# A two-layer hybrid diffusion backbone on one core: where the sliding heads' results are copied, how the weights lie in DRAM, and where the differential heads are normed

## What is computed

```
# one layer
h  = rmsnorm(x) * (1 + sc1) + sh1                 # modulation from silu(c) @ w_ada
p  = h @ w_in                                     # 1024 x 2304, nine pieces of 256 columns
ya = window attention, 8 heads of 64, GQA (2 kv heads), band of +-128 keys + 256 context keys + a sink
yb = gate * conv3(gate * p)                       # short convolution
yd = (softmax(q0 k0) - lam * softmax(q1 k1)) @ v  # 4 differential heads, 2 x 32 wide, over all keys
yd = rmsnorm(yd over its 64 columns, per head and token) * subln * (1 - lam_init)
x  = x + g1 * (concat(ya, yb, yd) @ w_out)
h2 = rmsnorm(x) * (1 + sc2) + sh2
x  = x + g2 * moe(h2)     # 16 experts, each takes its top 64 latent (32 context) tokens, SwiGLU, 3 x 4 MB
```

## Time and profile before

| | us |
|---|---|
| median of 3 runs | 2289.03 (2286.83 to 2295.98) |
| the profiled execution, as timed | 2285.29 |
| its span in the profile | 2283.5 |
| layer 0: attention steps | about 327 to 545 |
| layer 0: output projection to routing | about 565 to 701 |
| layer 0: experts | about 709 to 1247 |
| layer 1: W steps | about 1511 to 1618 |
| layer 1: experts | about 1739 to 2246 |

### The profile page before, as it was taken

One profiled execution on the slowest core, in us unless ns is written; L12 is line 12 of the kernel. 1 busy time (PEld: TensorE's weight loads), 2 busy tenths in 40 slices (PEclk: granted clock), 3 DMA queues, 4 the chain that ended last, 5 costly groups with the idle time before them and its releaser, 6 DMA issues.

```text
span 2283.5 us, 31609 instructions
## 1 busy us (share of the span) xinstructions
PE 1857.2 (81%) x13298; PEld 971.5 (43%) x13298; DVE 576.8 (25%) x1219; ACT 345.0 (15%) x753; POOL 260.4 (11%) x374
## 2 busy tenths in 40 slices
PE   4799978876976999999997689877785877777772
PEld 2677535564442444444333577456452222222220
DVE  1311236545233111111111221464333111101111
ACT  1210005453120000000000211255220000000001
POOL 1000004200000111211211000140000111101101
PEclk8999987798987999999999799799987999999997
DMA  9324880000235999999998612100134999999995
GB/s 331 106 93 166 313 331 1 1 1 29 83 129 188 380 391 384 390 385 389 385 390 315 226 56 74 37 1 1 47 138 186 391 390 397 396 392 391 396 402 198
DMA packets 170899, 530.85 MB, mean 232 GB/s; under 512 B 11780, under 2 KB 32544, under 8 KB 170784
## 3 DMA queue, kind: packets, MB, share of 16 engines
q1 hardware_dynamic: 150688, 480.28, 54.8%
q0 software_dynamic: 17488, 48.51, 7.4%
q10 hardware_dynamic: 2608, 0.35, 0.1%
HBM read 506.03 MB, written 23.07 MB: 232 GB/s over the span
## 4 chain that ended last, share of the span: by engine, by line
PE 58%; DMA 23%; DVE 10%; SPq 3%; ACT 3%; issue 2%; POOL 0%; ACTq 0%; DVEq 0%; POOLq 0%
PE psum L1156 12%; DMA ring<-in_w_gate 8%; DMA ring<-in_w_down 7%; PE psum L1089 6%; PE psum L1159 6%; DMA ring<-in_w_up 5%; PE psum L872 5%; PE psum L908 5%; PE psum L992 5%; PE psum L950 5%; DVE smx L1373 3%; PE psum L1150 3%; PE psum L1035 3%; SPq L472 3%; PE psum L826 2%
## 5 line engine op out<-in xcount | busy, mean ns | idle before, releaser
L1150 PE MATMUL psum<-ring,arena 128*64 128x512 f32 x1536 | 369.3, 607 | 118.2 <-DMA ring<-in_w_gate 48.7
L1156 PE MATMUL psum<-ring,arena 128*32 128x512 f32 x3072 | 403.0, 596 | 7.6 <-DVE arena L1506 2.2
L1150 PEld LDWEIGHTS psum<-ring,arena 128*64 128x64 f32 x1536 | 98.2, 137 | 366.8 <-issue 171.6
L1159 PE MATMUL psum<-ring,arena 128*32 128x256 f32 x3072 | 237.3, 380 | 0.0
L1159 PEld LDWEIGHTS psum<-ring,arena 128*32 128x32 f32 x3072 | 101.0, 110 | 230.3 <-issue 230.3
L794 ACT ACTIVATE arena<-psum 128x768 f32<-128x768 f32 (+1 forms) x32 | 22.5, 704 | 1018.3 <-PE psum L1159 522.2
L1373 DVE TENSOR_REDUCE smx<-psum 128x1 f32<-128x768 f32 (+4 forms) x160 | 120.7, 761 | 159.8 <-PE psum L1005 102.1
L731 ACT ACTIVATE arena<-psum,smx 128x768 f32<-128x768 f32 (+4 forms) x160 | 119.8, 751 | 266.3 <-DVE smx L1373 266.2
L1089 PE MATMUL psum<-ring,arena 128*128 128x512 f32 x320 | 144.1, 611 | 19.4 <-DVE arena L1421 19.4
L992 PE MATMUL psum<-arena 64*128 64x256 f32 (+3 forms) x640 | 119.9, 499 | 35.9 <-ACT arena L731 34.6
L1527 DVE SCALAR_TENSOR_TENSOR arena<-psum,gcur,arena 128x512 f32<-128x512 f32 x32 | 24.0, 750 | 460.3 <-PE psum L1159 233.3
(11 more groups left out here) (223 smaller groups left out, 1587.8 us busy)
## 6 DMA issues: line engine op xcount, KB each, us to landing
ring<-in_w_gate SPq DMA_DIRECT2D x128, 1024.0 KB, 4.7
ring<-in_w_up SPq DMA_DIRECT2D x128, 1024.0 KB, 18.5
ring<-in_w_down SPq DMA_DIRECT2D x128, 1024.0 KB, 20.0
ring<-in_w_ada SPq DMA_DIRECT2D x48, 1024.0 KB, 7.0
ring<-in_w_in SPq DMA_DIRECT2D x18, 1024.0 KB, 14.4
ring<-in_w_out SPq DMA_DIRECT2D x8, 1024.0 KB
arena<-residual POOLq DMA_DIRECT2D x14, 512.0 KB, 5.9
residual<-arena POOLq DMA_DIRECT2D x10, 512.0 KB, 2.9
```

Of the source, the lines that this page charges most:

```text
L1150: ins = mm(psum[64 * n:64 * n + 64, b * 512:(b + 1) * 512], lhs(k), w[:, n * 512:(n + 1) * 512], start=k == 0, stop=k == KD - 1)
L1156: ins = mm(psum[r0:r0 + 32, b * 512:(b + 1) * 512], lhs(k)[:, 32 * g:32 * g + 32], w[:, n * 512:(n + 1) * 512], start=k == 0, stop=k == KD ...
L1159: ins = mm(psum[32 * j:32 * j + 32, (b + 1) * 512:(b + 1) * 512 + 256], lhs_c(k), w[:, j * 256:(j + 1) * 256], start=k == 0, stop=k == KD - 1)
```

## The change

Three edits, and helpers for them.

- `by_partition` lays out `w_gate`, `w_up`, `w_down`, `w_out`, `w_ada` and `w_in` in DRAM before the launch, so that a unit's 8 KB for one partition are one run. The units, their order and the ring are as before.
- `mixed` of a W step moves from the end of DVE's iteration to its head.
- The norm of the differential heads goes into the W steps. POOL squares the differential results (1536 or 1024 columns) once all D copies are made. In `values` of W2 PE multiplies each block of squares by `halves`, now 128 x 2, so that tokens lie on partitions and a head's sum is one column (12 or 8 products); DVE copies the 24 or 16 columns, ACT takes the root, DVE the reciprocal. From W5 on, each of 2 x nq(l) steps broadcasts one block's gains through two small products and DVE applies them in `mixed`, just ahead of the copy (`dnorm`). What stood between attention and output projection for it is gone; the projection waits for `dnorm` instead of `dsub`.

```
+def by_partition(w, rows, cols=None):
+    k, n = w.shape[-2:]
+    cols = cols or n
+    lead = w.shape[:-2]
+    w = w.reshape(*lead, k // (rows * P), rows, P, n // cols, cols)
+    w = np.moveaxis(w, -2, -5) if cols < n else w[..., 0, :]
+    return np.ascontiguousarray(np.swapaxes(w, -3, -2))
...
+    SUMS_AT, GAIN_AT = 2, 5
+    def gain_chunk(l, st):
+        c = st.i - 4 * nq(l) - GAIN_AT
+        return divmod(c, 2) if st.kind == "W" and 0 <= c < 2 * nq(l) else None
+    def sums_here(l, st):
+        return st.i - 4 * nq(l) == SUMS_AT
... POOL, after its part of the D steps
+            pool.wait_ge(*L("mix", 2 * nq(l)))
+            pool.tensor_tensor(sqd[:, :, 0:tq], hT[:, 6:8, 0:tq], hT[:, 6:8, 0:tq], ALU.mult).then_inc(L["dsq"], 1)
... ACT, in iteration i behind the copy of the turned probabilities; its square and roots behind the steps are gone
+                    if i >= 5 and sums_here(l, steps[i - 5]):
+                        act.wait_ge(*L("dss", 1))
+                        act.activation(dms[:, 1, 0:nq(l)], dms[:, 0, 0:nq(l)], ACT.Sqrt, bias=eps[:]).then_inc(L["drt"], 1)
... PE, in values(st)
+                if sums_here(l, st):
+                    pe.wait_ge(*L("dsq", 1))
+                    for t in range(nq(l)):
+                        for cc in range(2):
+                            mm(psum[:, a0 + 256 + 4 * t + 2 * cc:a0 + 256 + 4 * t + 2 * cc + 2], sqd[:, cc, toks(t)],
+                               halves[:], start=True, stop=True)
+                if gain_chunk(l, st):
+                    t, cc = gain_chunk(l, st)
+                    pe.wait_ge(*L("dsr", 1))
+                    for h in range(2):
+                        mm(psum[64 * h:64 * h + 64, a0 + P:a0 + 2 * P],
+                           dms[:, 2, t, cc, h:h + 1].broadcast_to([P, HEAD]), ident[:], start=True, stop=True)
... PE, ahead of the output projection
-            pe.wait_ge(*L("dsub", 1))
+            pe.wait_ge(*L("dnorm", 2 * nq(l)))
... DVE, in mixed(st), ahead of its copy
+                if sums_here(l, st):
+                    dve.tensor_copy(dms[:, 0, 0:nq(l)]..., psum[:, a0 + 256:...]).then_inc(L["dss"], 1)
+                if gain_chunk(l, st):
+                    t, cc = gain_chunk(l, st)
+                    stt(hT[:, 6 + cc, toks(t)], hT[:, 6 + cc, toks(t)], sublc[:, l:l + 1], psum[:, a0 + P:a0 + 2 * P],
+                        ALU.mult, ALU.mult).then_inc(L["dnorm"], 1)
... DVE, head of iteration i
+                if i >= 5 and steps[i - 5].kind == "W":
+                    mixed(steps[i - 5])
+                if i >= 7 and sums_here(l, steps[i - 7]):
+                    dve.wait_ge(*L("drt", 1))
+                    dve.reciprocal(dms[:, 2, 0:nq(l)], dms[:, 1, 0:nq(l)]).then_inc(L["dsr"], 1)
... DVE, end of iteration i
-                if i >= 5 and steps[i - 5].kind == "W":
-                    mixed(steps[i - 5])
```

More of the change, by code:

```diff
@@ L200, in ada_units @@
     def ada_units(l, g):
-        v = w_ada[l].rearrange("(h k p) n -> h p k n", p=P, k=4)
-        return [(v[h, :, :, g * 512:(g + 1) * 512], 4) for h in range(2)]
+        return [(w_ada[l, g, h], 4) for h in range(2)]
     def win_units(l):
-        v = w_in[l].rearrange("(k p) n -> p k n", p=P)
         order = [0, 1, 2, 6, 7, 8, 3, 5, 4]
-        return [(v[:, :, 256 * j:256 * j + 256], 8) for j in order]
+        return [(w_in[l, j], 8) for j in order]
     def wout_units(l):
-        v = w_out[l].rearrange("(h k p) n -> h p k n", p=P, k=2)
-        return [(v[h], 2) for h in range(4)]
+        return [(w_out[l, h], 2) for h in range(4)]
     ADA_REST = [(0, g) for g in range(4, 12)] + [(l, g) for l in range(1, DEPTH) for g in range(12)]
@@ L339, in signals @@
         s |= dict.fromkeys("AV mix".split(), 6 * n)
+        s |= dict(dnorm=2 * n)
         s |= dict.fromkeys("cu cuc cy".split(), 2)
-        s |= dict.fromkeys("dsq dss drt dsub asub aexp aff aT pad rows ri".split(), 1)
+        s |= dict.fromkeys("dsq dss drt dsr asub aexp aff aT pad rows ri".split(), 1)
         s |= dict.fromkeys("xt xm xs gc silu he th hs yg".split(), NE)
@@ L464, in _ @@
                 n += 1
[L465 removed]
+            wv = [w[l] for w in (w_gate, w_up, w_down)]
             def load_matrix(which, expert, e, m0):
@@ L1057, in _ @@
                 ins.then_inc(L["gx"], 1)
[L1058 to L1063, removed]
             pe.wait_ge(*L("gxe", 1))
@@ L1204, in _ @@
         dlink(dve, dve.memset(halves[:], 0.0))
-        for h in (0, 64):
-            dve.memset(halves[h:h + 64, h:h + 64], 1.0 / HEAD)
+        for h in range(2):
+            dve.memset(halves[64 * h:64 * h + 64, h:h + 1], 1.0 / HEAD)
         dve.wait_ge(s_pack, 1)
@@ L1562 @@
     arrays = {f"in_{n}": np.ascontiguousarray(inputs[n]) for n in _INS}
+    for n in ("w_gate", "w_up", "w_down", "w_out"):
+        arrays[f"in_{n}"] = by_partition(inputs[n], 2)
+    arrays["in_w_ada"] = by_partition(inputs["w_ada"], 4, 512)
+    arrays["in_w_in"] = by_partition(inputs["w_in"], 8, 256)[:, :, 0]
     shape = inputs["x"].shape
```

28 lines of the change are left out of this document (9 added, 19 removed).

## The result

| | median, us | lowest to highest |
|---|---|---|
| before, 4 runs | 2292.22 | 2286.83 to 2295.98 |
| changed, 4 runs | 2220.84 | 2219.71 to 2223.30 |

The ratio is 0.9692 with an interval of 0.9667 to 0.9717, some 71 us. The profiled execution of the changed kernel was timed at 2219.7 us, its span is 2217.9. In the page after, these lines show most of it: first the chain's shares by engine, then packets and the SP queue (q1: packets, MB, share of 16 engines). DVE holds 7% of the chain (10% before), SP's issuing of loads (SPq) 0% (3% before), and q1 has 65952 packets for the same 480 MB; before it had 150688.

A forecast was written before the change was run, and what follows sets the result against it. PE bounds layer 0's experts, loads layer 1's, DVE's late copy the W steps. Savings 20.5 + 27.4 + 17.4 = 65.3 us give 2220 from the profiled 2285.3, 2223.7 from the median; forecast 2222, range 2203 to 2243.

The forecast's parts named there:

- rival A: All weight loads: they stay at their rate, limited by something other than runs; 2239 us, chance 0.22 together with D.
- rival B: W steps: another wait of the same length appears, so the early copy gives nothing; 2242 us, chance 0.08.
- W steps, layer 0: Attention steps with the early copy, norm work included: 12.3 us saved in layer 0, 8.2 in layer 1.
- tail, layer 0: Last copy to output projection, only gain broadcasts left there: 14.0 us saved in layer 0, 8.0 in layer 1.
- clock of the first 64 products: Output projection's start: without PE's pause before it, 64 products take 2 x 13.74 us, saving 2.9 and 2.5.
- runs: start, experts 0, experts 1: Weight loads in 8 KB runs, fixed cost 6.5 to 9.5 ns each: 1.6, 4.3 and 11.5 us saved.
- What is late next: W step after the early copy: PE's own work in a row, 4.5 us, or the exponentials, 4.3; the larger taken.
- sums: Products summing squares in W2's `values`, iteration W6: 24 passes cost 3.1 us in layer 0, 16 cost 2.0 in layer 1.
- The root: ACT's root with two table loads, some 2.8 us: 1.5 covered, 1.3 delays iteration W8's exponentials.
- POOL's square: POOL squaring 1536 columns before iteration W6: 4.4 us, at most 8.8, hidden by at least 12 us of cover.
- C: Experts of both layers: POOL's indirect transfers slowed by 8 KB runs, 2312 us if doubled, chance 0.03; small form 1 to 4.
- D: Weight loads: the edit doesn't reach the descriptors and runs stay 4 KB; 2239 us, counted within rival A's 0.22.

The follow-up runs named there:

- the changed kernel's second trace: The changed kernel run once more with no further edit, on the same chip as two later versions: 2221.07 us, ratio 0.9695 to before.
- copy and norm: Kernel before with the early copy and the norm in the W steps, weights still in 4 KB and shorter runs: 2238.78 us, ratio 0.9772.

## Why the prediction was right, step by step

The forecast was 2222.0, the result 2220.84. The total alone would prove little: the range of 2203 to 2243 also held the times given for rival A (2239) and rival B (2242). That the parts were right is shown by the runs of each part.

| term | predicted | measured |
|---|---|---|
| W steps, layer 0 | 12.3 | 12.3 |
| W steps, layer 1 | 8.2 | 8.8 |
| tail, layer 0 | 14.0 | 14.2 |
| tail, layer 1 | 8.0 | 8.1 |
| clock of the first 64 products | 2.9 and 2.5 | 2.7 and 2.3 |
| runs: start, experts 0, experts 1 | 1.6, 4.3, 11.5 | 2.9, 6.5, 10.8 |

The W steps are W5 to the last copy: 96.4 to 84.1 us and 70.5 to 61.8 (13.6 and 10.3 less by the changed kernel's second trace). The runs are means of all traces with 4 KB and with 8 KB.

- **The bound.** That a small copy at the end of DVE's iteration held every W step was right, and the copy alone shows it (34 us, no other edit). What is late next was right as well: PE in a row, 4.44 us for a forecast 4.5, and 4.6 with the gain for 4.8.
- **W6 to W8 were mis-sized, and other steps made up for it.** The sums took 3.15 us for 3.1 in layer 0 and 1.7 for 2.0 in layer 1. What failed is the step "sums": it priced the passes and not what PE's clock does behind them. `values` and `scores` ran at 0.50, and W7 took 5.8 us where the sum had 4.3. The gains cost 0.37 us each for a forecast 0.3, but the steps with them came out 0.2 us shorter than put down, and those with four key blocks 4.25 for 4.6. The total of layer 0 fits by such cancelling, which is luck, not because each step was known.
- **The root.** Put down as 1.3 us uncovered for each layer; without it each layer is 1.4 shorter.
- **POOL's square** was taken for hidden, which holds, at 2.91 us where my row of a one-operand scaling gave 4.4. That it holds DVE still for as long I had not seen; it lies on the chain in one trace, but taking it away shortened nothing.
- **The tail** was right to 0.2 us in both layers, the clock term too: the first 64 products took 27.66 us in both.
- **The runs.** The fixed cost of a run was right (7.5 ns for a forecast 6.5 to 9.5), and so was layer 1. Layer 0's experts were put at the 4.3 us of PE's idle time in one stretch, "no more"; the stage gave 6.5. Over the whole stage PE stood still for 16.6 us before and for 13.2 in the changed kernel, 3.3 less, and was busy for 528.7 us in place of 531.3 with the same 6368 matmuls. With the runs alone it stood still 3.2 us less and was busy 0.4 less. So the idle time came back nearly as forecast, and the rest is in PE's own work, for a reason that the rows don't show. The start gave 2.9 for 1.6.
- **Where the medians hide a difference.** The profiled execution before (2285.3) was 6.9 us under the median of all four runs before, that of after 1.1 under its own. Between the two spans lie 65.6 us, close to the 65.3 of the sum; between the medians 71. The forecast of 2222 took its starting point between that execution and the median, and the median then rose from 2289.0 to 2292.2 with the fourth run; an error of 1.2 us in the total is smaller than these. The terms as measured add to 68.6, so the sum was some 3 us short, mostly in the runs.
- **Rivals.** A fell with the runs alone, B with the copy alone. C is there in its small form: the indirect transfers land 1.7 and 0.9 us later, 2.6 together for a forecast 1 to 4, and in the kernel with only the runs likewise (10.3 and 7.8). D fell with the packets of q1.

## What to carry to other kernels

Look at what stands last in an engine's iteration and is waited for first by another engine: moving a copy of 0.2 us from the tail of DVE's list to its head was worth more than the whole norm behind the steps, and it decided how much moving that norm paid (5 us alone, 17 on top of the early copy, by the medians). Where a stage is bound by loads, count the runs as well as the bytes: here each run cost 7.5 to 8.7 ns on its engine, and a layout made before the launch took half of the experts' away at no cost in the measured time. PE's work that is slipped into a step that PE bounds is priced in full (0.37 us for each gain), and the narrow products did better here in small groups; look at the granted clock behind them.

## What the hardware showed that I had not expected

- **PE's clock fell with a row of narrow products.** 24 passes with two moving columns in a row, PE busy throughout: granted clock 0.85 and then 0.50 over 5 us, 0.92 and 0.72 in another trace of the same kernel. In three groups of eight between other work: 1.00, and each pass 0.10 us in place of 0.13. What decides how far it falls, these runs don't tell.
- **DVE stands still beside POOL.** A scaling of 128 x 512 on DVE took 2.97 us beside a POOL product of 2.91, and 0.48 otherwise; with the square on ACT the longest was 0.55.
- **Longer runs, more in flight, and SP free.** A load of `w_down` landed 14.8 us after its issue with 2 KB runs, 20.3 with 4 KB (copy and norm) and 29.8 with 8 KB in a stretch of layer 1's experts, though the stretch moved more bytes each time. Times the rate this is an estimate of 5.6, 8.0 and 11.9 MB on the way; only the last is nearly the whole ring. SP's rows fit that. At the program's start, with 2 KB runs, its first three loads took 0.43 to 0.56 us each to issue and the next four 2.6 to 3.2; with 8 KB seven in a row took under 0.45 each. SP's issuing is 5% of the chain with 2 KB runs in the experts, 3% before and 0% in the changed kernel. What holds SP up is not shown, nor whether it has a price beside that of the runs where the engines aren't full.
- **Equal code, two lengths.** Layer 1's attention took 161.9 us in one trace of the changed kernel and 165.2 in the other, and 180.2 against 183.7 in two kernels whose attention is that of before. The difference lies up to W5: 96.6 against 100.1, and 95.1 against 100.1. From W5 on it is 83.6 and 83.6, and 66.7 against 65.2, the sums' clock. Thirteen traces have three lengths up to W5, 95.1, 96.7 and 100.1 us, without regard to the kernel, and in layer 0 two, 121.9 and 122.6. A gain of a few us in one trace of these stages has to be read step by step.
